# An mLSTM and stick-breaking trunk on eight cores: the sums of x, the first head's groups and the gate prologue rearranged, transposes planned with other due times

## The chip, the cores and the metric

The kernel runs on all 8 cores of one Trainium2 chip. Each core works on one of the 8 sequences of the batch and exchanges nothing with the others. The metric is the device time in microseconds (us) of the slowest core.

## The reference, cut to what matters

Two layers act on x of 2048 tokens by 2048 features per core.

Layer A (mLSTM, 8 heads): `u = x @ w_in` gives per head q and k (128 columns each), v (256), the output gate o and the SiLU gate z (256 each), and once for all heads 16 gate columns. q and k go through a causal convolution of width 4 and SiLU. The gate columns give a log input gate and a log forget gate per token and head; their running maxima and sums scale a chunkwise recurrence (here 16 chunks of 128 tokens per head) that mixes q, k and v. The result is normalised per head, multiplied by `sigmoid(o) * silu(z)`, projected by `w_out`, added to `alpha * x`, and layer-normalised.

Layer B (stick-breaking attention, 16 heads) projects queries, a SiLU gate and one shared set of keys and values, forms sigmoid scores with a running product along the keys, and ends with a projection, the residual and a layer norm.

## The kernel before, in words

**The planner.** The program is written as some 40 generators ("streams", all handed to `Sched.run`), each of which yields operations in its own order, with conditions between them. The planner keeps an estimated clock for each engine and for each tile (last written, last read) and emits, of all streams' next operations, the one whose estimated start is earliest; an operation marked `first=True` wins a tie. So the estimates don't move the hardware: they fix the order of the instructions in each engine's queue. The engines then run their queues in that order and wait by semaphores for true dependences. `slack` is added to the estimated end of whatever an operation waits for on another engine, so an operation with slack is put later in its queue. For DMAs (`KB.dma`) there is one estimated DMA clock `tdma`: each transfer, transposes too, starts after the one before it and takes `cost`; its destination counts as written, and its source as free, `lat` later. Transposes have `lat=LATE`, 14; all others 1.2.

**Queues.** Weights and x come by DMAs that GpSimd (POOL) issues, since they convert float32 to bfloat16. Transposes and stores are issued by SyncE (SP). Both queues are in order like any other.

**Layer A's beginning.** x arrives transposed in four blocks of 512 tokens, `XT[0..3]`. `plain` (matmul at L556) makes q, k and v of head 0 from it in the ordinary way: 4 x 64 matmuls of 512 columns into four PSUM banks, evicted by `pev` (L579). In between, `prologue` (L486) makes the gate columns of a block; after the fourth block it works out the gates for all heads: a chain that alternates between TensorE (L503, L507, L511, L513, L529) and VectorE (L505, L506, L509, L517, 32 dependent operations on one partition at L522 and L524, L526), with exponentials on ScalarE at L498, L500 and L535 to L538. Only after it (`st["pro"]`) may the recurrence of any head begin.

**Groups.** Every other projection of layer A is done by `grp` with 7 instead of 8 products (a Strassen form). A group is (head, pair pr of weight blocks, token half p): pr 0 is q and k, 1 is v, 2 and 3 are o and z. Weight pair `w = 4h + pr` sits in slot `w % 3` of `RW`; its loading starts once pair w-3 is done (`wd`). A group is 7 products of 8 matmuls (L608), 56 in all. Its operands are sums of weight quarters (`wsum`, L451: three on VectorE and two on POOL per pair) and sums of quarters of x (`xsum`, once per half p = 0, 1): three new tensors `FX` (L425, VectorE, 128x4096 bf16 each), two negations in place (L428, ScalarE) and two subtractions in place (L432, on POOL for p = 0, on VectorE for p = 1). `grp` waits until all seven of its half are in the queues (`at("xsum") >= p`), and `xsum` itself waits until all plain products and gates of the half are. The order is by the list `GL`: for head 0, whose q, k and v are already made, (o, p 0), (o, p 1), (z, p 0), (z, p 1). `gev` evicts a group (L626 to L683), with three subtractions or additions on VectorE.

**Beside the groups.** `conv` (L713 to L727) makes q and k of a head; `kn` transposes k, `vtr` transposes v by DMA; `knw` (L783), `recf` (L794), `recm` (L808 to L827) and `reco` (L840 to L853) do the recurrence chunk by chunk; `hbt` transposes its output by DMA into one of 12 tiles `HT`; `htg` (L869) multiplies by the gates that `gat` (L757 to L773) has made and stores to `mida`. The gates of head h+1 may overwrite those of head h only when the store of the same token block is issued. All DMAs have the line L162. After the last head the output projection of layer A starts (L941, tiles REGX and REGW), then layer B (L1104, L1185, L1212, L1238, L1270) and its output projection (L941 again, tiles REGH and REGX).

## Time and profile before

| what | us |
|---|---|
| three runs: median (lowest to highest) | 2592.64 (2577.12 to 2977.39) |
| profiled execution, device time | 2585.65 |
| its span, first to last instruction of the slowest core (core 3) | 2584.0 |
| spans of the eight cores | 2555.9 to 2584.0 |
| TensorE, VectorE, ScalarE, GpSimd busy in the span | 2439.5, 1729.4, 1031.0, 1262.1 |

The profiled execution's device time lies 1.65 us above its span. A window row of the profile gives, for one stretch of the span, the busy time and the number of records of each engine (PE is TensorE, DVE VectorE, ACT ScalarE), the granted TensorE clock as a share of full speed, the busy share of the DMA engines, and GB/s.

### The profile page before, as it was taken

To read this page: it belongs to the slowest core of one execution; us is meant where nothing else is said; L and a number is where in the kernel's file an instruction comes from. 1 tells how busy PE (TensorE), PEld (TensorE's weight loads), DVE (VectorE), ACT (ScalarE), POOL (GpSimd) and SP (SyncE) were. 2 spreads that over 40 slices of the span, in tenths; PEclk is the share of its full clock that TensorE was granted. 3 is DMA by queue.
4 is the path that set the end of the run, shared out by engine and by line. 5 is a ranking of instruction groups with operands and counts; after the bars stand their busy time and mean duration, and the time that the engine had idled before them with its cause. 6 is when DMAs were issued, how large, how long until landed. Compare 5 with 4: busy or idle time off the path is not lost.

```text
span 2584.0 us, 37351 instructions; the slowest of 8 cores (2555.9 to 2584.0 us)
## 1 busy us (share of the span) xinstructions
PE 2439.5 (94%) x11811; PEld 1127.4 (44%) x11811; DVE 1729.4 (67%) x2859; ACT 1031.0 (40%) x1877; POOL 1262.1 (49%) x1099
## 2 busy tenths in 40 slices
PE   7599899999999989999899999999999999998997
PEld 3244344444444444444344444444444444443443
DVE  2686687777778757664567766666666677565765
ACT  1455455555555532323334443433334444431111
POOL 2565465647557433433445544555444555442533
PEclk9799999999999989999899999999999999999998
DMA  9559766976567577973466576667767766686762
GB/s 155 81 80 89 107 101 108 111 122 111 96 113 113 93 255 231 252 216 80 111 114 134 105 131 113 124 118 122 123 114 109 115 109 102 133 195 175 252 202 82
DMA packets 518142, 342.35 MB, mean 132 GB/s; under 512 B 453184, under 2 KB 486080, under 8 KB 505536
## 3 DMA queue, kind: packets, MB, share of 16 engines
q1 hardware_dynamic: 492688, 214.06, 39.2%
q0 software_dynamic: 25264, 125.91, 27.7%
q8 instruction: 101, 1.65, 0.3%
q14 instruction: 89, 0.73, 0.1%
HBM read 272.82 MB, written 83.89 MB: 138 GB/s over the span
## 4 chain that ended last, share of the span: by engine, by line
PE 71%; DVE 11%; DMA 8%; POOL 4%; issue 4%; ACT 1%; SPq 1%; another core or an unknown queue 0%; DVEq 0%; POOLq 0%; ACTq 0%
PE PSA L1104 25%; PE PSA L608 19%; PE PSA L941 16%; PE PSA L1270 4%; DVE REGW L1212 4%; DMA REGX<-REGW 3%; PE PSA L1185 3%; DMA REGW<-a_wu 2%; PE PSA L556 2%; POOL REGW L1238 1%; DMA REGH<-REGX 1%; DVE REGW L451 1%; SPq L162 1%; DVE REGW L869 1%; DMA REGX<-x_t 1%
## 5 line engine op out<-in xcount | busy, mean ns | idle before, releaser
L1104 PE MATMUL PSA<-REGH,REGX 128*128 128x512 bf16 x4096 | 975.2, 380 | 5.9 <-DVE REGW L1111 5.9
L1212 DVE TENSOR_TENSOR_SCAN REGW<-PSA,REGW 128x512 f32<-128x512 f32 (+3 forms) x640 | 685.8, 1091 | 301.5 <-ACT PSA L1190 235.3
L1238 POOL TENSOR_TENSOR REGW<-REGW 128x1024 bf16<-128x1024 f32 (+7 forms) x384 | 526.9, 1389 | 354.0 <-DMA REGX<-REGW 185.0
L1104 PEld LDWEIGHTS PSA<-REGH,REGX 128*128 128x128 bf16 x4096 | 397.5, 98 | 461.6 <-issue 10.3
L1190 ACT ACTIVATE PSA<-PSA 128x512 f32<-128x512 f32 (+3 forms) x640 | 326.3, 519 | 304.0 <-PE PSA L1185 298.3
L608 PE MATMUL PSA<-REGX,REGW 128*128 128x512 bf16 x1680 | 405.8, 379 | 4.4 <-issue 3.6
L608 PE MATMUL PSA<-REGH,REGW 128*128 128x512 bf16 x1680 | 404.2, 382 | 0.0
L1116 ACT CAST REGW<-PSA 128x512 bf16<-128x512 f32 x192 | 112.7, 587 | 336.6 <-PE PSA L1104 334.9
L608 PEld LDWEIGHTS PSA<-REGH,REGW 128*128 128x128 bf16 x1680 | 163.8, 98 | 177.6 <-issue 4.7
L608 PEld LDWEIGHTS PSA<-REGX,REGW 128*128 128x128 bf16 x1680 | 160.9, 98 | 174.9 <-issue 5.9
L1185 PE MATMUL PSA<-REGW 128*128 128x512 bf16 (+3 forms) x640 | 220.1, 350 | 15.2 <-DVE REGW L1212 14.7
L941 PE MATMUL PSA<-REGH,REGX 128*128 128x512 bf16 x1024 | 223.8, 381 | 3.0 <-DVE REGW L944 2.0
L941 PE MATMUL PSA<-REGX,REGW 128*128 128x512 bf16 x1024 | 223.4, 382 | 0.0
L451 POOL TENSOR_TENSOR REGW<-REGW 128x1024 bf16<-128x1024 bf16 x60 | 132.4, 2212 | 58.2 <-DVE REGW L451 58.1
L848 POOL TENSOR_TENSOR REGW<-REGW,SM 128x1 f32<-128x1 f32 x128 | 76.9, 601 | 170.4 <-DVE REGW L846 153.4
L941 PEld LDWEIGHTS PSA<-REGH,REGX 128*128 128x128 bf16 x1024 | 100.5, 98 | 124.9 <-issue 5.9
L941 PEld LDWEIGHTS PSA<-REGX,REGW 128*128 128x128 bf16 x1024 | 100.7, 98 | 122.3 <-issue 2.7
L727 POOL TENSOR_TENSOR REGX<-REGW 128x512 bf16<-128x512 f32 x64 | 90.0, 1406 | 121.1 <-ACT REGW L725 82.0
L1270 PE MATMUL PSA<-REGX,REGW 128*128 128x512 bf16 (+3 forms) x640 | 130.6, 351 | 17.0 <-DMA REGX<-REGW 15.4
L964 ACT ACTIVATE REGW<-REGW,BMVB 128x2048 f32<-128x2048 f32 x26 | 54.3, 2093 | 229.4 <-DVE BMVB L958 229.4
L721 DVE SCALAR_TENSOR_TENSOR PSA<-REGW,PRT,PSA 128x512 f32<-128x512 f32 x128 | 96.1, 750 | 51.6 <-ACT PSA L715 49.7
L944 DVE SCALAR_TENSOR_TENSOR REGW<-REGW,PSA 128x512 f32<-128x512 f32 x108 | 73.9, 684 | 74.4 <-PE PSA L941 63.1
(144 smaller groups left out, 2440.5 us busy)
## 6 DMA issues: line engine op xcount, KB each, us to landing
REGW<-a_wu POOLq DMA_DIRECT2D x64, 512.0 KB, 8.1
y<-REGW SPq DMA_DIRECT2D x26, 1024.0 KB, 5.2
REGX<-wb POOLq DMA_DIRECT2D x32, 512.0 KB, 4.5
REGW<-y SPq DMA_DIRECT2D x14, 1024.0 KB, 7.6
REGW<-x SPq DMA_DIRECT2D x13, 1024.0 KB, 6.6
wao<-a_w_out POOLq DMA_DIRECT2D x32, 256.0 KB, 6.9
mida<-REGW SPq DMA_DIRECT2D x128, 64.0 KB, 2.8
wb<-kv_w POOLq DMA_DIRECT2D x32, 256.0 KB, 6.4
```

Of the source, the lines that this page charges most:

```text
L451: yield Op(e, lambda: E.tensor_tensor(out=out[0], in0=i0[0], in1=i1[0], op=op), R=i0[1] + i1[1], W=out[1], cost=x)
L608: yield Op("pe", lambda: P_.matmul(PS[bank], lhsT=wo[0][:, c, :], rhs=xo[0][:, c, :], start=(k == 0 and c == 0), stop=(c == 7), skip_group ...
L721: yield Op("dve", lambda: V.scalar_tensor_tensor(out=pc if k else acc, in0=U[u][:, k:k + 512], scalar=wk(k), in1=pc, op0=ALU.mult, op1=ALU ...
L727: yield Op("pool", lambda: G.tensor_tensor(out=dst[:, tb * 512:(tb + 1) * 512], in0=acc, in1=sig, op=ALU.mult), R=ak + gk, W=[dk[tb]], cos ...
L941: yield Op("pe", lambda: P_.matmul(PS[bank], lhsT=mg(c), rhs=wo[:, c, :], start=(c == 0), stop=(c == KC - 1)), R=mgk + wok, W=[("ps", bank ...
L1104: yield Op("pe", lambda c=c: P_.matmul(PS[bank], lhsT=WS[i % 4][:, c, :], rhs=X1[tb][:, c, :], start=(c == 0), stop=(c == KC - 1)), R=[f"W ...
L1116: yield Op("act", lambda: A_.copy(out=dstT[:, tsl], in_=PS[bank]), R=[("ps", bank)], W=[key], cost=0.6, first=True)
L1185: yield Op("pe", lambda: P_.matmul(PS[bank][:, 0:w], lhsT=QTs[par][:, (n - 1) * 128:n * 128], rhs=KTs[par][:, b0 * 128:b1 * 128], start=Tr ...
L1190: yield Op("act", lambda: A_.activation(out=PS[bank][:, 0:w], in_=PS[bank][:, 0:w], func=AF.Sigmoid, scale=-scale), R=[("ps", bank)], W=[( ...
L1212: yield Op("dve", lambda: V.tensor_tensor_scan(out=RR[slot][:, lo:hi][:, ::-1], data0=PS[bank][:, 0:w][:, ::-1], data1=mk[:, ::-1], initia ...
L1238: yield Op("pool", lambda: G.tensor_tensor(out=AA[:, (pos + b0) * 128:(pos + b1) * 128], in0=RR[slot][:, lo + 1:hi + 1], in1=RR[slot][:, l ...
L1270: yield Op("pe", lambda: P_.matmul(PS[bank][:, f0:512], lhsT=VVs[par][:, sb_, :], rhs=TT[:, gp + sb_, f0:512], start=(sb_ == 0), stop=(sb_ ...
```

## The change

It has eight parts.

1. `xsum`: the three new sums of a half are no longer held until all its plain products and gates are in the queues; each is held only until the first plain product of the last block that it reads is. The two subtractions of half 0 move from POOL to VectorE. None of the seven is `first` any more. Each enters a set `xs` by itself.
2. `grp`: a product waits for the one sum of x that it reads, `(p, k) in xs`, not for all seven.
3. `GL`: head 0's groups run (o, p 0), (z, p 0), (o, p 1), (z, p 1).
4. `wsum`: for weight pairs 2 and 3 all five sums are on VectorE.
5. `prologue`: five TensorE steps after the gates have slack 4.0 instead of 0.3.
6. `LATE` is 16 instead of 14.
7. `KB.dma`: transposes get an estimated clock of their own, `tsp`; they no longer delay, nor are delayed by, other transfers. A source counts as free `min(lat, 8)` after the transfer, the destination as written `lat` after it.
8. `hbt`: the output transposes have `lat` 32 for heads 0 to 6 and 12 for head 7.

```diff
-LATE = 14.0
+LATE = 16.0
+SLK = 4.0
...
-        self.tdma = max(self.tdma, start + 1.2) + cost
-        self._time(self.tdma + lat, R, W)
+        if lat > 1.2:
+            self.tsp = end = max(self.tsp, start + 1.2) + cost
+        else:
+            self.tdma = end = max(self.tdma, start + 1.2) + cost
+        self._time(end + min(lat, 8.0), R, ())
+        self._time(end + lat, (), W)
...
-            go = [(h, 2, 0), (h, 2, 1), (h, 3, 0), (h, 3, 1)] if h < NH_A - 1 else [(h, 2, 0), (h, 3, 0), (h, 2, 1), (h, 3, 1)]
+            go = [(h, 2, 0), (h, 2, 1), (h, 3, 0), (h, 3, 1)] if 0 < h < NH_A - 1 else \
+                [(h, 2, 0), (h, 3, 0), (h, 2, 1), (h, 3, 1)]
...
-                yield lambda: at("qkp") >= 4 * b + 3 and at("gates") >= b
...
-                for out, i0, i1, op in ((fx(0), b11, b22, ALU.add), (fx(2), b21, b11, ALU.subtract), (fx(1), b12, b22, ALU.subtract)):
+                for i, out, i0, i1, op, tb in ((1, fx(2), b21, b11, ALU.subtract, a), (0, fx(0), b11, b22, ALU.add, b),
+                                               (4, fx(1), b12, b22, ALU.subtract, b)):
+                    yield lambda: at("qkp") >= 4 * tb
...
-                             cost=2.3, first=True)
-                for x in (b22, b11):
...
+                             cost=2.3)
+                    xs.add((p, i))
+                yield lambda: at("qkp") >= 4 * b + 3 and at("gates") >= b
+                for i, x in ((2, b11), (3, b22)):
...
-                e, E, x = ("dve", V, 2.3) if p else ("pool", G, 7.5)
...
+                for i, out, i1 in ((5, b21, b22), (6, b12, b11)):
+                    yield Op("dve", lambda: V.tensor_tensor(out=out[0], in0=out[0], in1=i1[0], op=ALU.subtract), R=i1[1], W=out[1],
+                             cost=2.3)
+                    xs.add((p, i))
...
-                    e, E, x = ("pool", G, 2.2) if j > 2 else ("dve", V, 0.65)
+                    e, E, x = ("pool", G, 2.2) if j > 2 and w > 3 else ("dve", V, 0.65)
...
-                     R=["TRIU", "SPF"], W=[("ps", 6)], cost=0.25, slack=0.3)
+                     R=["TRIU", "SPF"], W=[("ps", 6)], cost=0.25, slack=SLK)
...
-                yield lambda: ((need is None and (3, pb) in evs or need in evd) and (w, sums) in ws and at("xsum") >= p)
+                yield lambda: ((need is None and (3, pb) in evs or need in evd) and (w, sums) in ws and (p, k) in xs)
...
-                         dma=dict(slot=f"ht{i % NHT}", out=HT[i % NHT], in_=HB[i % 4], transpose=True, lat=LATE))
+                         dma=dict(slot=f"ht{i % NHT}", out=HT[i % NHT], in_=HB[i % 4], transpose=True, lat=2 * LATE if i < 112 else LATE - 4))
```

## Rows read from the trace of the kernel before

**Rows 1.** The page, part 1 (TensorE's line), and spans of two cores
```profile
PE 2439.5 (94%) x11811; PEld 1127.4 (44%) x11811; DVE 1729.4 (67%) x2859; ACT 1031.0 (40%) x1877; POOL 1262.1 (49%) x1099
...
core 1: 2555.9 us, clock 0.983
...
core 3: 2584.0 us, clock 0.981
```

**Rows 2.** Line L941, layer A's output projection, core 1, then core 3
```profile
L941 PE MATMUL PSA<-REGX,REGW x1024: 379/379/631, 919.8 to 1142.9; 128*128 128x512 bf16 x171
...
L941 PE MATMUL PSA<-REGX,REGW x1024: 379/379/634, 944.7 to 1167.7; 128*128 128x512 bf16 x171
```

**Rows 3.** Windows of core 3, and last one of core 1
```profile
77.60:140.00 62.40, 31.88 (x131) 13.90 (x132) 51.22 (x97) 23.49 (x36) 26.80 (x17) 0.75 0.36 59
140.00:240.00 100.00, 98.45 (x489) 46.78 (x488) 75.81 (x196) 53.90 (x109) 57.45 (x64) 1.00 0.76 95
240.00:280.00 40.00, 27.73 (x121) 12.22 (x120) 17.74 (x48) 14.63 (x29) 18.92 (x18) 0.87 1.01 69
920.00:945.00 25.00, 16.55 (x81) 7.76 (x80) 15.08 (x53) 11.58 (x23) 9.80 (x12) 0.81 0.94 296
...
240.00:280.00 40.00, 40.00 (x202) 19.23 (x200) 31.93 (x83) 21.21 (x44) 29.77 (x30) 1.00 0.69 125
```

**Rows 4.** Timeline of TensorE: start, length, instructions [idle before, what ended it]
```profile
55.42 13.97 PE L556 MATMUL PSA<-REGH,REGW 128*128 128x512 bf16 x64
...
72.47 3.61 PE L556 MATMUL PSA<-REGH,REGW 128*128 128x512 bf16 x16
...
76.14 1.46 PE L556 MATMUL PSA<-REGH,REGW 128*128 128x512 bf16 x6
88.53 0.45 PE L507 MATMUL PSA<-ID,REGW 128*128 128x128 f32 x1 [10.94 <-DVE REGW L506]
...
101.44 1.19 PE L529 MATMUL PSA<-REGW,ONE 1*128 1x128 f32 x4 [8.05 <-DVE REGW L526]
...
111.71 0.59 PE L608 MATMUL PSA<-REGX,REGW 128*128 128x512 bf16 x2
...
120.20 0.27 PE L810 MATMUL PSA<-REGW 128*128 128x257 bf16 x1 [2.18 <-DVE REGW L797]
...
126.90 0.27 PE L794 MATMUL PSA<-REGX 128*128 128x128 bf16 x1 [6.08 <-ACT REGW L853]
```

**Rows 5.** Windows of L556 alone, then of L608 alone, TensorE and weight loads
```profile
77.60:140.00 62.40, 13.01 (x42) 4.58 (x42) 0.75 0.36 59
...
77.60:140.00 62.40, 15.57 (x61) 6.29 (x62) 0.75 0.36 59
```

**Rows 6.** Timeline of VectorE around the sums
```profile
56.64 6.69 DVE L425 TENSOR_TENSOR REGX<-REGX 128x4096 bf16<-128x4096 bf16 x3
...
72.65 0.62 DVE L495 TENSOR_TENSOR REGW<-PSA,REGW 128x128 f32<-128x128 f32 x2 [7.80 <-PE PSA L486]
...
77.93 8.01 DVE L451 TENSOR_TENSOR REGW<-REGW 128x1024 bf16<-128x1024 bf16 x3 [4.67 <-DMA REGW<-a_wu]
...
103.85 1.89 DVE L451 TENSOR_TENSOR REGW<-REGW 128x1024 bf16<-128x1024 bf16 x3
```

**Rows 7.** Line L451 on VectorE until 140 us: duration ns min/median/max, starts
```profile
L451 DVE TENSOR_TENSOR REGW<-REGW x7: 679/683/5739, 77.9 to 133.7; 128x1024 bf16<-128x1024 bf16 x7
```

**Rows 8.** Timeline of GpSimd
```profile
67.30 15.82 POOL L432 TENSOR_TENSOR REGX<-REGX 128x4096 bf16<-128x4096 bf16 x2 [10.78 <-ACT REGX L428]
...
90.38 0.59 POOL L162 DMA_DIRECT2D REGW<-a_wu  x1 [2.25 <-PE PSA L556]
```

**Rows 9.** Timelines of SyncE and ScalarE, then transposes of 200 to 300 us by median landing
```profile
237.46 9.93 SPq L162 DMA_TRANSPOSE REGH<-REGX  x1
...
269.64 0.40 ACT L783 ACTIVATE REGW<-REGH,REGW 128x128 bf16<-128x128 bf16 x1 [17.75 <-DMA REGH<-REGX]
...
REGW<-REGH SPq DMA_TRANSPOSE x8, 12.7
```

More of the change, by code:

```diff
@@ L507, in prologue @@
             yield Op("pe", lambda: P_.transpose(out=PS[7][:, 0:128], in_=AL, identity=ID32[:]), R=["AL", "ID32"],
-                     W=[("ps", 7)], cost=0.25, slack=0.3)
+                     W=[("ps", 7)], cost=0.25, slack=SLK)
             yield Op("dve", lambda: V.tensor_reduce(out=SM[:, 1:2], in_=PS[7][:, 0:128], axis=AX.X, op=ALU.max),
@@ L511, in prologue @@
             yield Op("pe", lambda: P_.matmul(PS[6][0:1, 0:128], lhsT=SM[:, 1:2], rhs=ID32[:], start=True, stop=True),
-                     R=["SM1", "ID32"], W=[("ps", 6)], cost=0.25, slack=0.3)
+                     R=["SM1", "ID32"], W=[("ps", 6)], cost=0.25, slack=SLK)
             yield Op("pe", lambda: P_.matmul(PS[6][0:1, 128:256], lhsT=ONE32[:, 0:1], rhs=SPF, start=True, stop=True),
@@ L529, in prologue @@
                 yield Op("pe", lambda: P_.matmul(PS[7][:, 128 * i:128 * i + 128], lhsT=ONE32[0:1, :], rhs=rw[:, 2 + i, :],
-                                                 start=True, stop=True), R=["ONE32", "ROW"], W=[("ps", 7)], cost=0.25, slack=0.3)
+                                                 start=True, stop=True), R=["ONE32", "ROW"], W=[("ps", 7)], cost=0.25, slack=SLK)
             yield Op("dve", lambda: V.tensor_tensor(out=TMP, in0=AL, in1=PS[7][:, 0:128], op=ALU.subtract),
```

11 lines of the change are left out of this document (4 added, 7 removed).

## The prediction, made before the changed kernel was run

> **What bounds the kernel now.** I read the busy shares first: TensorE is busy 94% of the span [rows 1], so the time is TensorE's work plus its holes. Next the spans of the cores: they do equal work, yet core 1 takes 2555.9 us and core 3, which sets the metric, 2584.0 [rows 1]. The first matmul of L941 ends layer A. On core 1 it starts at 919.8, on core 3 at 944.7 [rows 2]; from there to the end of the span it is 2555.9 - 919.8 = 1636 and 2584.0 - 944.7 = 1639 us. So all the spread arises in layer A, which is also all that the change touches, and the forecast can be made as: (start of L941 on the slowest core) + 1639 + 1.65 us around the span.
>
> Then windows of layer A [rows 3]. From 77.6 to 140 us TensorE is busy 31.88 of 62.40 us at a granted clock of 0.75. From 140 to 240 it is busy 98.45 of 100. From 240 to 280 core 3 loses 12.3 us, core 1 nothing. At the end, 920 to 945, 8.45 us are idle. So the beginning is the largest hole, and it is on every core.
>
> The timeline of TensorE names the waits of the beginning [rows 4]. By 77.6, 22 of the last block's 64 plain products are done (16 and 6). The 42 others are ready to run, but behind them in the queue's order come steps of the gate prologue: 10.94 us before L507, 8.05 before L529, both for VectorE. The first group's product starts at 111.71. Later 2.18 and 6.08 us (and 3.3 in two smaller ones) go to the recurrence, held while VectorE makes the sums of half 1. Why VectorE was late: its weight sums L451 take 8.01 us for three [rows 6]; their usual time is 0.683 us, but one took 5.739 [rows 7]. It began at 77.93 and ended near 83.7, just behind GpSimd's two subtractions, 67.30 to 83.12 [rows 8].
>
> **The change, part by part.**
>
> *Ceiling of the beginning.* Idle: 62.40 - 31.88 = 30.5 us [rows 3]. Slow clock: a plain product takes 13.97 / 64 = 0.218 us at full clock [rows 4]. The 42 plain ones took 13.01 instead of 9.2, the 61 of groups 15.57 instead of 13.3 [rows 5]: 6.1 us. Ceiling 36.6 us; no more can come from parts 1 to 5.
>
> *Sums of x (1, 2).* Each of the ten VectorE operations costs 6.69 / 3 = 2.23 us [rows 6]. For half 0 the three new sums used to run at 56.6 to 63.3 [rows 6] and can now go ahead of 56, where VectorE is mostly idle; its two subtractions, new on VectorE, cost 4.5 us and follow the negations, near 60 to 67. They lie beside plain products and cost nothing. For half 1, three new sums (6.7 us) can go at about 67 to 77, into the 7.80 and 4.67 us in which VectorE waited [rows 6]. If that cover is gone they fall on the prologue. Half 1's rest is 4.5 us behind its gates. Since a product waits only for its own sum, group 0 needs nothing of this that is late.
>
> *Weight sums (4).* Two pairs of two sums move to VectorE: 4 x 0.68 = 2.7 us. The 5.74 us operation goes back to 0.68 as the long subtractions leave GpSimd: -5.1 us. Pair 2 is complete at about 77.9 + 5 x 0.68 = 81.3. The Trainium skill (SBUF — State Buffer, "SBUF: two separate sides") says that VectorE and GpSimd take one pair of ports as an exclusive lock, the loser blocked for the whole instruction. The 5.74 us agree with that. By the same rule the sums moved to VectorE can block, or be blocked by, GpSimd's shorter multiplications; no term of my sum uses it.
>
> *Prologue slack (5).* A step is now put 4 us instead of 0.3 behind what it waits for, so plain products are issued ahead of it. VectorE can have its L506 result at about 81.3 + 1 = 82.3, against 76 + 5 = 81 by the planner's distance: a wait of about 1 us remains, between 0 and the 11 of before. The price is that the recurrence starts no earlier than now (L529 at 101) rather than earlier; while it is late, groups run.
>
> *Group order (3).* The 42 plain products from 77.6 end at 77.6 + 9.2 = 86.8, so group 0 can start near 87 instead of 111.7. A group is 56 x 0.218 = 12.2 us: group 1 at 99, group 2 at 111, group 4 at 136. Group 1 now needs pair 3. Its load waits for pair 0's last product; that was 90.38 [rows 8] and becomes about 80 to 81. Before, the pair's first sums ran at 103.85 [rows 6], 13.5 us behind the first load's issue; with that as an upper end and 3.4 for five sums it is ready by 98, 1 us ahead of need. If it came 5 us late, group 1 would lose 4; that is inside the range. Group 2 needs half 1's sums at 111, ready near 90. Pair 5's load starts after group 2 instead of group 1, 12 us later, and is needed 24 us after that: hidden.
>
> *Is VectorE able to follow?* This is what can eat the gain. Up to the work that is done by 240 us, VectorE is busy 51.22 + 75.81 = 127.0 us from 77.6 on [rows 3]. The change takes off 5.1 (block) and 6.7 (sums of half 1 made earlier), adds 2.7: 117.9 us. TensorE, given back its whole ceiling, would reach that work at 240 - 36.6 = 203.4, leaving VectorE 125.8 us: a busy share of 94%. In the crowded window before it had 51.22 / 62.40 = 82%. At 82% it would need 143.7 us, until 221.3, and the gain would be 18.7; at 94% all of 36.6. What VectorE does late is chiefly the recurrence, which may lag some chunks behind the groups without stopping TensorE, so I take a value nearer the ceiling: 30 us, bounds 18.7 and 36.6.
>
> *Due times in the steady part (6, 7, 8).* The trace shows no planned times, so these are bounds. In heads 1 to 7 TensorE has little left to give: 1.55 us in the 100 of the second window [rows 3]. Best: the hole of 240 to 280 goes too. It is 12.3 us idle and 27.73 x 0.13 = 3.6 of slow clock, 16 us. SyncE spent 9.93 us issuing one transpose at 237.46, and the k weighting on ScalarE waited 17.75 us for its landing [rows 9]. Worst: such a hole comes more often (rival 3). In a quiet queue a transpose is now due 2 us later than before; next to loads it is due earlier, as the planner no longer puts the loads' time in front of it. The rows show this collision of transposes and loads on core 3 only once, so I take 0, bounds -16 and +16. `lat` 32 for the output transposes puts L869 and the stores later in the queues; in tiles it has room (12 of them, against about 6.5 us per chunk), and nothing on TensorE waits for them until the end.
>
> *The tail (8).* Head 7's are due at 12 instead of 14, and no longer behind the three large loads of `w_out`. Between 0 and 8.45 us [rows 3] could go; the row shows work on the recurrence itself in that time, so 0.
>
> Sum: 2585.65 - 30 = 2555.65, say **2556 us**. The profiled execution lies 0.3% under the median shown, 2592.64, and between the other two runs' ends; I forecast against it.
>
> **The rivals.**
>
> 1. *VectorE takes TensorE's place at the beginning.* For it: 82% was the most it reached in 62 us, and every queue is in order. Against: its other 11.2 us there [rows 3] were mostly waits for TensorE's late steps, and those go. Time: 2585.65 - 18.7 = 2567.
> 2. *The hole at 240 us goes as well.* For it: core 1 has none in the same program, and the change shifts loads against transposes. Against: nothing in it thins the loads. Time: 2585.65 - 30 - 16 = 2540.
> 3. *Transposes planned too early next to loads: slower than before.* With a clock of their own, k and v transposes are planned as if no load ran. The rows show 12.7 us median landing for the v transposes of 200 to 300 us on core 3 and an issue of 9.93 [rows 9]. A TensorE step planned at such a due time stands in front of group products and stops them, 16 us each time. At one hole more per core, half of the 30 is gone; from two more on (-30 + 32) the kernel is slower. With three more in the seven heads: 2585.65 - 30 + 48 = 2604. Against: the due time was only roughly right before too, and one hole came of it. [...]
> 4. *The order doesn't change where it counts.* The planner may still estimate pair 2 or the gates so that the old order comes out. Against: slack and per-product conditions act on just the steps that waited. Time: 2586.
>
> **How the numbers follow.** Forecast 0.52, rival 1 0.20, rival 2 0.13, rival 3 0.08, rival 4 0.07. The forecast's own range is 2542 to 2570. Low end: 2585.65 - 36.6 - 16 - 8.45 = 2525 (say 2526); high end: rival 4 with some scatter of the runs, 2592, which leaves out rival 3. A measurement of this kernel can tell about 2% from no change, 2541 and 2644 here. Faster by over 2% are half of rival 2 and a tenth of the forecast: 0.11. Slower by over 2% is the far end of rival 3: 0.02. Within 2%: 0.87.
>
> **What would show it.** Right: TensorE's busy share from 77.6 to 140 above 0.9 at full granted clock; L608's first start near 87; waits before L507 and L529 under 2 us each; no VectorE L451 of 5 us; L432 four times on VectorE at 2.3 us; group products done by 140 near 210; L941 first starting near 915 on the slowest core and 890 on the best; 1639 us from there. Rival 1 would show as waits of TensorE for VectorE between 100 and 240, rival 3 as waits of ScalarE's L783 or TensorE for DMA in several heads. The forecast is wrong if L941 starts later than 935 on the slowest core, or if the part behind L941 changes.

## The result: slower, and where the profile shows it

Over 15 executions each, the kernel before had a median of 2572.76 us (2565.06 lowest) and the changed kernel 2622.51 us (2600.75 lowest). The ratio of the runs compared is **1.0166, 95% interval 1.0142 to 1.0190**. The forecast was 2556 us, in a range of 2526 to 2592; the result lies outside it, on the other side of the kernel before. Runs that were disturbed on a whole die are left out of all ratios here.

The profiled execution of the changed kernel took 2600.75 us. It was the fastest of its 15, while the profiled one of before (2585.65) lay above its median. So the two traces differ by only 15 us where the ratio says some 40; the traces tell where time goes, the ratios how much, and what the changed kernel loses in its slower executions no trace here shows. The page and the spans of the two cores of [rows 1]:

```profile
PE 2444.6 (94%) x11811; PEld 1127.0 (43%) x11811; DVE 1736.0 (67%) x2865; ACT 1033.4 (40%) x1879; POOL 1232.0 (47%) x1093
...
core 1: 2587.9 us, clock 0.985
...
core 3: 2599.1 us, clock 0.982
```

Most lines of the kernel moved down by 9: L608 is now L617 (groups), L556 L565, L503 L512, L507 L516, L529 L538, L451 L460, L853 L862, L869 L878, L941 L950. L162 and L432 are L167 and L440. In the experiments without part 7 they lie 1 to 4 lines higher. Layer A's output projection on core 3, against 944.7 in [rows 2]:

```profile
L950 PE MATMUL PSA<-REGX,REGW x1024: 379/379/634, 955.5 to 1184.1; 128*128 128x512 bf16 x171
```

For every core I split the span at three events: the first group product, the last one, and the first output-projection product. Medians over the eight cores, us:

| kernel | first group | groups' stretch | tail | behind it | span |
|---|---|---|---|---|---|
| before | 111.3 | 810.8 | 11.7 | 1638.3 | 2571.1 |
| changed | 91.8 | 841.9 | 7.9 | 1641.2 | 2582.2 |

The columns are, in order: start of the first group product, from it to the last one, from there to the first product of the output projection, from there to the end, and the whole.

**The beginning did gain; the groups lost more than that.** They start 19.5 us sooner and then take 31.1 us longer. Both halves show in the windows of core 3, the first three of which answer to [rows 3]; the last row of the fence behind it is the kernel before over the long steady stretch:

```profile
77.60:140.00 62.40, 53.91 (x243) 24.06 (x242) 47.68 (x111) 35.62 (x55) 22.73 (x22) 0.92 0.41 66
140.00:240.00 100.00, 85.71 (x421) 40.36 (x418) 67.77 (x183) 47.43 (x99) 50.99 (x58) 0.96 0.85 99
240.00:280.00 40.00, 33.19 (x161) 15.53 (x162) 34.13 (x91) 20.36 (x41) 23.66 (x26) 0.90 0.58 88
...
280.00:880.00 600.00, 565.48 (x2763) 265.72 (x2762) 465.39 (x1121) 305.30 (x618) 336.78 (x365) 0.99 0.69 105
```

```profile
280.00:880.00 600.00, 585.42 (x2897) 277.39 (x2895) 475.10 (x1178) 320.57 (x650) 358.42 (x385) 1.00 0.69 110
```

TensorE is busy 22.0 us more up to 140 us, 12.7 less in the next hundred, and 19.9 less from 280 to 880. No single wait of the steady stretch is large; that is why it must be read by windows and groups of waits.

**Beginning, core 3.** L565 alone, then L617 alone, from 77.6 to 140 us, against [rows 5]; then TensorE, VectorE and ScalarE in the timelines, against [rows 4, 6]:

```profile
77.60:140.00 62.40, 11.31 (x44) 4.41 (x42) 0.92 0.41 66
...
77.60:140.00 62.40, 40.86 (x171) 16.78 (x172) 0.92 0.41 66
```
```profile
83.01 0.46 PE L512 MATMUL PSA<-REGW 128*128 128x128 f32 x2 [2.75 <-ACT REGW L509]
...
91.79 1.89 PE L617 MATMUL PSA<-REGX,REGW 128*128 128x512 bf16 x8
99.42 2.29 PE L617 MATMUL PSA<-REGX,REGW 128*128 128x512 bf16 x5 [5.74 <-ACT PSA L635]
```
```profile
80.57 4.28 DVE L460 TENSOR_TENSOR REGW<-REGW 128x1024 bf16<-128x1024 bf16 x5
```
```profile
92.17 1.28 ACT L734 ACT_TABLE_LOAD   x1 [7.50 <-DVE REGW L730]
...
95.18 3.61 ACT L437 ACTIVATE REGH<-REGH 128x4096 bf16<-128x4096 bf16 x1
98.69 0.58 ACT L635 COPY PSA<-PSA 128x512 f32<-128x512 f32 x1
```

The waits of 10.94 and 8.05 us before L507 and L529 (L516, L538) are gone, and so is the 5.74 us weight sum; 2.75 us are left before L512. By 140 us 171 group products have run where there had been 61: 110 x 0.218 = 24 us of lead. A new wait of 5.74 us stands in the first group. Its eviction L635 sits in ScalarE's queue behind a table load and the 3.61 us negation L437 of half 1's sums. VectorE has a part in it: ScalarE had stood 7.50 us for VectorE's L730, which came behind five weight sums (4.28 us from 80.57) and these two sums of half 1:

```profile
84.77 4.49 DVE L432 TENSOR_TENSOR REGH<-REGH 128x4096 bf16<-128x4096 bf16 x2
```

**Head 1, core 3.** Part of the chain of waits, then lines of VectorE's, TensorE's and SyncE's timelines:

```profile
215.88 26.53 DMA REGW<-a_wu
```
```profile
242.43 0.69 DVE L460 TENSOR_TENSOR REGW<-REGW 128x1024 bf16<-128x1024 bf16 x1 [15.38 <-DMA REGW<-a_wu]
```
```profile
244.51 0.27 PE L803 MATMUL PSA<-REGX 128*128 128x128 bf16 x1 [15.19 <-ACT REGW L862]
```
```profile
216.60 12.53 SPq L167 DMA_TRANSPOSE REGW<-REGH  x1
...
234.39 11.24 SPq L167 DMA_TRANSPOSE REGW<-REGH  x1
```

A weight load issued at 215.88 took 26.5 us to land, beside transposes whose issue alone took 12.5 and 11.2 us. VectorE had the pair's first sum next in its queue and stood for 15.4 us; the recurrence's steps behind it, and so TensorE, stood too. It is the hole of [rows 3] with another victim: there a transpose was late for ScalarE, here a load for VectorE. From 200 to 280 us TensorE is idle 12.4 us in the mean over the cores, where it was 7.0 before.

**Heads 2 to 7, core 0.** TensorE's recurrence lines between 280 and 880 us, first before, then changed. The last part is idle time ahead of them and what ended it (the same lines, 9 apart):

```profile
L808 PE MATMUL PSA<-REGW 128*128 128x257 bf16 x92 | 25.1, 273 | 3.2 <-DVE REGW L822 2.2 <-ACT REGW L783 0.7
L810 PE MATMUL PSA<-REGW 128*128 128x257 bf16 x92 | 25.1, 273 | 6.6 <-DVE REGW L797 4.8 <-DVE REGW L841 1.6
...
L794 PE MATMUL PSA<-REGX 128*128 128x128 bf16 x91 | 19.9, 219 | 0.6 <-ACT REGW L853 0.3
```
```profile
L819 PE MATMUL PSA<-REGW 128*128 128x257 bf16 x87 | 23.8, 274 | 8.4 <-DVE REGW L806 7.1 <-DVE REGW L854 0.8 <-DVE REGW L859 0.3
L817 PE MATMUL PSA<-REGW 128*128 128x257 bf16 x86 | 23.5, 273 | 8.8 <-DVE REGW L831 8.1 <-ACT REGW L792 0.8
...
L803 PE MATMUL PSA<-REGX 128*128 128x128 bf16 x86 | 18.8, 219 | 5.5 <-ACT REGW L862 5.3
```

10.4 us became 22.7: 3.2 + 6.6 + 0.6 against 8.4 + 8.8 + 5.5. Most of it is for VectorE, and the 5.3 for ScalarE's L862 too come from its waiting for VectorE's L859 (46.7 us in all there). Two pictures from head 4 of that core show why VectorE is late. The first is a load that VectorE waits for; the second, operations of two engines that hold each other up:

```profile
585.37 0.69 DVE L460 TENSOR_TENSOR REGW<-REGW 128x1024 bf16<-128x1024 bf16 x1 [3.03 <-DMA REGW<-a_wu]
...
586.60 0.27 PE L817 MATMUL PSA<-REGW 128*128 128x257 bf16 x1 [1.78 <-DVE REGW L831]
```
```profile
596.62 3.18 DVE L878 TENSOR_TENSOR REGW<-REGW 128x256 bf16<-128x256 bf16 x2
...
597.48 2.17 POOL L460 TENSOR_TENSOR REGW<-REGW 128x1024 bf16<-128x1024 bf16 x1
...
601.58 0.27 PE L819 MATMUL PSA<-REGW 128*128 128x257 bf16 x1 [1.69 <-DVE REGW L806]
```

Two small multiplications that otherwise take 0.48 us took 3.18, beside the end of a GpSimd multiplication (L773, until 597.51) and GpSimd's sum. From these rows I formed the theory for the experiments: *with the new due times the order of the queues is wrong by some microseconds in every head; VectorE's next instruction waits for a load, or meets a long GpSimd operation, and the recurrence stands behind it.* The idle time in heads 2 to 6 supports it: most of it lies at the same four chunks. At chunk 15 it is 1.2 to 1.7 us in every head and on every core; at chunks 6, 8 and 12 the mean over the cores is 0.1 to 2.4 us by head, with none on some cores. A fixed order gives such a pattern; chance alone would not.

### The profile page after: what moved, and what is told of

The parts are those of the page before. It is cut to its first block, busy times and chain, and to the rows that moved or that the text cites. A ratio compares the mean times of both kernels' runs of the same rounds, so it can differ in the third digit from the quotient of the medians.

```text
span 2599.1 us, 37395 instructions; the slowest of 8 cores (2566.7 to 2599.1 us)
## 1 busy us (share of the span) xinstructions
PE 2444.6 (94%) x11811; PEld 1127.0 (43%) x11811; DVE 1736.0 (67%) x2865; ACT 1033.4 (40%) x1879; POOL 1232.0 (47%) x1093
## 4 chain that ended last, share of the span: by engine, by line
PE 71%; DVE 12%; DMA 8%; issue 4%; POOL 3%; ACT 2%; SPq 1%; DVEq 0%; POOLq 0%; ACTq 0%
PE PSA L1113 26%; PE PSA L617 18%; PE PSA L950 16%; DVE REGW L1221 5%; PE PSA L1279 4%; PE PSA L1194 3%; DMA REGW<-REGW 3%; DMA REGW<-a_wu 2%; DMA REGX<-REGW 2%; PE PSA L565 1%; DMA REGX<-x_t 1%; DVE REGW L878 1%; POOL REGW L1247 1%; SPq L167 1%; DVE REGW L460 1%
## 5 line engine op out<-in xcount | busy, mean ns | idle before, releaser
L617 PE MATMUL PSA<-REGX,REGW 128*128 128x512 bf16 x1680 | 406.5, 382 | 6.0 <-ACT PSA L635 5.7
L617 PE MATMUL PSA<-REGH,REGW 128*128 128x512 bf16 x1680 | 407.7, 382 | 2.8 <-DVE REGW L859 2.8
L617 PEld LDWEIGHTS PSA<-REGX,REGW 128*128 128x128 bf16 x1680 | 162.9, 98 | 178.9 <-issue 12.7
L617 PEld LDWEIGHTS PSA<-REGH,REGW 128*128 128x128 bf16 x1680 | 162.8, 98 | 177.4 <-issue 6.1
L950 PE MATMUL PSA<-REGX,REGW 128*128 128x512 bf16 x1024 | 223.9, 382 | 5.1 <-DVE REGW L953 5.1
L950 PE MATMUL PSA<-REGH,REGX 128*128 128x512 bf16 x1024 | 223.8, 381 | 2.4 <-DVE REGW L953 1.5
L736 POOL TENSOR_TENSOR REGX<-REGW 128x512 bf16<-128x512 f32 x64 | 84.4, 1319 | 165.7 <-ACT REGW L734 111.6
L950 PEld LDWEIGHTS PSA<-REGX,REGW 128*128 128x128 bf16 x1024 | 100.8, 99 | 128.0 <-issue 8.9
L950 PEld LDWEIGHTS PSA<-REGH,REGX 128*128 128x128 bf16 x1024 | 100.4, 98 | 124.4 <-issue 5.5
L1279 PE MATMUL PSA<-REGX,REGW 128*128 128x512 bf16 (+3 forms) x640 | 130.6, 351 | 15.5 <-DMA REGX<-REGW 13.8
L460 POOL TENSOR_TENSOR REGW<-REGW 128x1024 bf16<-128x1024 bf16 x56 | 123.5, 2205 | 29.0 <-DVE REGW L460 28.8
L862 ACT ACTIVATE REGW<-PSA,REGW 128x256 bf16<-128x256 f32 x128 | 71.6, 559 | 118.7 <-DVE REGW L859 102.7
```

Of the source, the lines that this page charges most:

```text
L460: yield Op(e, lambda: E.tensor_tensor(out=out[0], in0=i0[0], in1=i1[0], op=op), R=i0[1] + i1[1], W=out[1], cost=x)
L617: yield Op("pe", lambda: P_.matmul(PS[bank], lhsT=wo[0][:, c, :], rhs=xo[0][:, c, :], start=(k == 0 and c == 0), stop=(c == 7), skip_group ...
L736: yield Op("pool", lambda: G.tensor_tensor(out=dst[:, tb * 512:(tb + 1) * 512], in0=acc, in1=sig, op=ALU.mult), R=ak + gk, W=[dk[tb]], cos ...
L950: yield Op("pe", lambda: P_.matmul(PS[bank], lhsT=mg(c), rhs=wo[:, c, :], start=(c == 0), stop=(c == KC - 1)), R=mgk + wok, W=[("ps", bank ...
L1279: yield Op("pe", lambda: P_.matmul(PS[bank][:, f0:512], lhsT=VVs[par][:, sb_, :], rhs=TT[:, gp + sb_, f0:512], start=(sb_ == 0), stop=(sb_ ...
```

## The experiments

Ratios are to the kernel before, with their 95% intervals. "Parts 1 to 5 alone" (e1) is the base of most.

### Halves of the change

e1 is the changed kernel without parts 6, 7, 8:

```diff
-LATE = 16.0
+LATE = 14.0
...
-        if lat > 1.2:
-            self.tsp = end = max(self.tsp, start + 1.2) + cost
-        else:
-            self.tdma = end = max(self.tdma, start + 1.2) + cost
-        self._time(end + min(lat, 8.0), R, ())
-        self._time(end + lat, (), W)
+        self.tdma = max(self.tdma, start + 1.2) + cost
+        self._time(self.tdma + lat, R, W)
...
-                         dma=dict(slot=f"ht{i % NHT}", out=HT[i % NHT], in_=HB[i % 4], transpose=True, lat=2 * LATE if i < 112 else LATE - 4))
+                         dma=dict(slot=f"ht{i % NHT}", out=HT[i % NHT], in_=HB[i % 4], transpose=True, lat=LATE))
```


> Parts 1 to 5 alone: the due times of transposes (LATE 14, one DMA clock, output transposes like all) are those of before. Theory 1 (the new due times cost time in heads 1 to 7, the new beginning gains its share): first group product near 92 us as in the changed kernel, waits of TensorE for the recurrence from 280 us on as short as before (about 10 us instead of 25), time 0.99 to 0.995 of before. Theory 2 (the lead won at the beginning is itself what disturbs the later heads, through VectorE or through the order of the queues): first group product near 92, but the later heads as slow as in the changed kernel, time 1.01 to 1.02 of before.

e2 is the kernel before with exactly these lines changed the other way (parts 6, 7, 8 alone).

> Parts 6 to 8 alone on the kernel before. Theory 1: the beginning as before (first group product near 111 us), longer waits of TensorE in heads 1 to 7, time 1.02 to 1.03 of before, slower than the changed kernel. Theory 2: the time of before within 0.5%.

e1: **0.9923** [0.9878, 0.9967]; e2: **1.0081** [1.0058, 1.0103]. The beginning's parts make the kernel faster, the due times make it slower, and that settles where the sign comes from. The stage table: e1 97.5 / 793.8 / 11.7 / 1638.3, e2 101.9 / 824.8 / 7.5 / 1649.1. e1's groups take 17 us less than before, e2's 14 us more. The split is not clean: the due times alone (e2) also start the groups 9.4 us sooner, and behind the groups e2 loses 10.8 us. The product of the two ratios is 1.000, the whole is 1.0166; 1.6% are an interaction.

### One part of the due times taken away from the changed kernel

e3 takes the last edit of e1's diff alone (part 8 undone), e4 the middle one alone (part 7 undone).

> The changed kernel without part 8: the output transposes are due LATE (16) after their transfer for all heads, not 32 and 12. If part 8 is what costs (products and stores L878 put late in VectorE's queue, gates held up behind them): the time falls to 0.99 to 1.00 of before. If part 7 or the beginning costs: it stays within 0.5% of the changed kernel, 1.012 to 1.02.

> The changed kernel without part 7: one estimated DMA clock for transposes and loads, sources free as late as destinations are written; LATE 16 and the 32 and 12 of part 8 stay. If transposes planned too early beside loads are what costs (rival 3 of the prediction): the time falls to 0.99 to 1.00 of before. If not: it stays at 1.012 to 1.02, or rises a little, since output tiles count as busy for 32 us more.

e3: 1.0049 [1.0010, 1.0089]; e4: **1.0468** [1.0418, 1.0518]. So part 8 costs, and removing part 7 alone is far worse than keeping it. In e4 the output transposes have `lat` 32 and their source tile `HB`, of which there are four, counts as taken for 32 us. The planner then spaces the recurrence by it. Core 0 of e4, TensorE from 280 to 880 us:

```profile
L815 PE MATMUL PSA<-REGW 128*128 128x257 bf16 x76 | 22.8, 300 | 44.5 <-DVE REGW L802 43.4 <-DVE REGW L846 0.5 <-DVE REGW L855 0.4
...
L799 PE MATMUL PSA<-REGX 128*128 128x128 bf16 x75 | 17.4, 232 | 15.2 <-ACT REGW L858 15.2
```

Part 8 can stand only where a source is freed apart from the landing, as part 7 does (8 us) and as e10 below does (14 us); the three parts can't be judged one at a time.

### One part of the due times added to parts 1 to 5

e5 and e11 change `LATE` alone, to 16.0 (part 6) and 15.0. e6 adds the whole of part 7. e7 adds only its early release of the source, e8 only the clock of its own, e10 part 8 with the sources free after 14 as in e1:

```diff
 e7
+        self.tdma = end = max(self.tdma, start + 1.2) + cost
+        self._time(end + min(lat, 8.0), R, ())
+        self._time(end + lat, (), W)
 e8
+        if lat > 1.2:
+            self.tsp = end = max(self.tsp, start + 1.2) + cost
+        else:
+            self.tdma = end = max(self.tdma, start + 1.2) + cost
+        self._time(end + lat, R, W)
 e10
+        self._time(self.tdma + min(lat, 14.0), R, ())
+        self._time(self.tdma + lat, (), W)
...
+                         dma=dict(slot=f"ht{i % NHT}", out=HT[i % NHT], in_=HB[i % 4], transpose=True, lat=32.0 if i < 112 else 12.0))
```


> The new beginning with the due times of before, but LATE 16 (part 6 alone of the three). If 2 us more on every transpose cost nothing, the time is that of the beginning alone, 0.985 to 0.997 of before, the groups' stretch about 794 us (median over cores, first to last group product). If a due time that is later costs much by itself (LATE is part of what made the groups' stretch 842 in the changed kernel), the stretch is over 810 and the time above 1.0.

> The new beginning with LATE 14 and part 7 whole: a DMA clock of its own for transposes, and sources free 8 us after the transfer. If part 7 is what made the groups' stretch long (rival 3 of the prediction, in this or that form), it is 820 to 840 and the time about 1.0 to 1.01 of before; if LATE 16 was, it is about 794 and the time 0.99.

> The new beginning with LATE 14, one DMA clock as before, but sources counted as free min(lat, 8) after the transfer instead of lat (half of part 7). If the early release is what costs (the output chunks HB are written, and with them the recurrence steps of TensorE are placed, as if the transposes had read their sources 6 us sooner), the groups' stretch is over 815. If the separate clock costs, it stays near 794.

> The new beginning with LATE 14, sources free as late as before, but a DMA clock of its own for transposes (the other half of part 7). If transposes planned as if no load ran are what costs, the groups' stretch is over 815 and there are more waits for transposes to land; if the early release costs, it stays near 794.

> The new beginning with the due times of before, and part 8 alone: output transposes due 32 (head 7: 12) after their transfer instead of 14, their sources still free after 14. Part 8 was seen to cost about 8 us of the groups' stretch on top of parts 6 and 7. If that is additive: groups' stretch about 802 us, time 0.995 to 1.0 of before. If each part costs its whole alone, as parts 6 and 7 did (any departure from the old order costs): stretch 815 or more, time 1.0 or more.

> The new beginning with LATE 15, half way to part 6. If the time follows the due time smoothly: between 0.992 and 1.001 of before. If what decides is the chance of how the planner's order falls (VectorE's operations against GpSimd's that block them), it can lie outside, 1.005 or 0.987 as well.

| run | ratio | interval | groups' stretch |
|---|---|---|---|
| e1 base | 0.9923 | 0.9878 to 0.9967 | 793.8 |
| e11, LATE 15 | 0.9922 | 0.9895 to 0.9950 | 790.8 |
| e5, LATE 16 | 1.0014 | 0.9973 to 1.0055 | 814.7 |
| e6, all of part 7 | 1.0031 | 1.0002 to 1.0060 | 827.4 |
| e7, early release | 1.0060 | 1.0024 to 1.0095 | 838.8 |
| e8, own clock | 1.0055 | 1.0020 to 1.0090 | 827.7 |
| e10, part 8 | 0.9980 | 0.9952 to 1.0009 | 808.2 |

Parts 6 and 7, and either half of part 7, take the whole gain back, each on its own. For part 8 the intervals of e10 and e1 overlap; its groups' stretch is 14 us longer. The waits for DMAs from 280 to 880 us on core 0 show how; columns are the total, how often, the longest. First e7, then e8, then the changed kernel without part 8 (e3):

```profile
DVE REGW L457 <- DMA REGW<-a_wu: 25.2, 9, 8.0
ACT REGW L859 <- DMA REGW<-REGW: 12.1, 4, 3.9
```
```profile
ACT REGW L791 <- DMA REGH<-REGX: 18.3, 3, 8.1
DVE REGW L459 <- DMA REGW<-a_wu: 17.5, 8, 3.9
```
```profile
ACT REGW L862 <- DMA REGW<-REGW: 32.5, 6, 15.5
```

Before and in e1 there is one such row, weight loads:

```profile
DVE REGW L451 <- DMA REGW<-a_wu: 8.0, 8, 1.8
```
```profile
DVE REGW L456 <- DMA REGW<-a_wu: 3.0, 4, 1.2
```

With early release (e7, e3) ScalarE is told to write `HB` (L859, L862) while the transpose still reads it. With an own clock (e8) the k weighting (L791) stands before its transpose has landed. In both, the loads' sums stand too early on VectorE: 25 and 17.5 us against 3.0. The k weighting's wait is not found in the changed kernel: there L792 waits for no transpose between 280 and 900 us, on any core.

### The loads, and both due times moved back

Both start from the changed kernel. e9 has the first edit (the planned length of a weight load), e13 both:

```diff
-                yield Op("pool", None, W=rwk[s][2 * u:2 * u + 2], cost=3.0,
+                yield Op("pool", None, W=rwk[s][2 * u:2 * u + 2], cost=4.5,
...
-        self._time(end + min(lat, 8.0), R, ())
+        self._time(end + min(lat, 14.0), R, ())
```

> The changed kernel, with a weight load planned at a cost of 4.5 instead of 3.0 us, so that the weight sums (VectorE, in order) are put later. Theory: part 7 took the transposes out of the loads' estimated clock, weight sums are now put in VectorE's queue before their weights have landed, and what is behind them (the recurrence, then TensorE) waits. Then VectorE's waits for a_wu in heads 2 to 7 fall from 15 us to about 7 (kernel before: 6), the idle time of TensorE there from 31 to about 23, the time to 1.005 to 1.01 of before. Rival, that the transposes' own due times or GpSimd's blocking of VectorE are the cause: the waits for a_wu fall, but the idle time and the time stay (1.012 or more).

> The changed kernel with weight loads planned at 4.5 us as before this, and with the sources of transposes counted as free 14 us after the transfer instead of 8. Theory: two kinds of waits on DMAs made the later heads long, VectorE's weight sums for a_wu, and ScalarE's output chunk (L862) for the transpose that still reads its tile. Both should now be near 0 and TensorE's idle time in heads 2 to 7 fall from 31 us (25 without the first) to 10 to 15, the time to 0.995 of before. If it stays at 24, DMA waits are not the second half, and GpSimd's blocking of VectorE or the order itself is.

e9: 1.0062 [1.0034, 1.0090]; e13: 1.0090 [1.0060, 1.0119]. e9's edit did what it should: the waits for `a_wu` between 280 and 900 us are gone (16.8 us on core 0 before the edit), and a percent comes back. e13's second edit did not: ScalarE's L862 still waits 5.6 us for transposes in the mean over the cores (6.2 in the changed kernel), though the blocked sums shrink. Means over the cores (us), the first three from the first group product of head 2 to the last of head 7: TensorE idle, VectorE waiting for `a_wu`, what VectorE's weight sums take above 0.683 us each; then TensorE waiting in layer A's output projection for `mida`, which it reads back:

| kernel | idle | waits for a_wu | sums' excess | wait for mida | ratio |
|---|---|---|---|---|---|
| before | 10.9 | 6.4 | 9.1 | 0 | 1 |
| changed | 31.7 | 14.9 | 16.5 | 0 | 1.0166 |
| e1 | 11.7 | 7.1 | 8.9 | 0 | 0.9923 |
| e2 | 34.1 | 19.8 | 14.6 | 0 | 1.0081 |
| e10 | 20.8 | 6.5 | 12.5 | 0 | 0.9980 |
| e11 | 7.7 | 5.1 | 18.2 | 0 | 0.9922 |
| e9 | 25.0 | 0.0 | 12.7 | 18.7 | 1.0062 |
| e13 | 17.1 | 0.5 | 3.5 | 17.0 | 1.0090 |
| e12 (below) | 8.3 | 4.3 | 2.1 | 0 | 0.9882 |

Neither cause alone sets the idle time: e9 has no wait for a load left and 25.0 us idle, and e11 has the largest excess of the table and the least idle time. That the two together make up the holes is therefore argued from the rows above, not shown.

e13 cures some two thirds of what the steady part had lost, yet its ratio is no better than e9's. One reason stands in the last stage. Both kernels reach the output projection early and then stand in it, on every core by 14.8 to 21.6 us. TensorE and SyncE of core 0 in e9:

```profile
920.59 3.61 PE L950 MATMUL PSA<-REGX,REGW 128*128 128x512 bf16 x16 [1.42 <-DMA REGW<-mida]
943.94 4.42 PE L950 MATMUL PSA<-REGX,REGW 128*128 128x512 bf16 x10 [19.73 <-DMA REGW<-mida]
...
935.91 2.49 SPq L167 DMA_DIRECT2D REGW<-mida  x3
```

Three of its reads of `mida` are issued at 935.91 only, behind transposes and stores in SyncE's queue, when the projection has already begun. In the kernel before, core 0, they were issued by 927.2 and the projection began at 935.6. So what the edits win in the heads is partly paid again here; the planned length of a load moves this order too. e8 has 7.8 us of the same wait. The other reason is a lower clock, see e17 below.

### The slack, the order of groups, the engines of the sums

e12 and e18 are e1 without the added slack (parts 1 to 4 alone), e14 is e12 with `LATE` 15.0, e16 is e12 without part 3, e17 is the changed kernel without the added slack. e15 is the kernel before with only the two engine choices of parts 1 and 4:

```diff
-SLK = 4.0
+SLK = 0.3
...
-            go = [(h, 2, 0), (h, 2, 1), (h, 3, 0), (h, 3, 1)] if 0 < h < NH_A - 1 else \
+            go = [(h, 2, 0), (h, 2, 1), (h, 3, 0), (h, 3, 1)] if h < NH_A - 1 else \
...
-                e, E, x = ("dve", V, 2.3) if p else ("pool", G, 7.5)
+                e, E, x = ("dve", V, 2.3)
...
-                    e, E, x = ("pool", G, 2.2) if j > 2 else ("dve", V, 0.65)
+                    e, E, x = ("pool", G, 2.2) if j > 2 and w > 3 else ("dve", V, 0.65)
```


> The new beginning with the due times of before, without part 5: the prologue's TensorE steps have slack 0.3 again. By the prediction part 5 frees the plain products: without it two waits come back, before the second and the last prologue step, smaller than 10.9 and 8.1 us since VectorE's weight sum is no longer blocked; about 10 us together, first group product at about 105 instead of 98, time about 0.4% above the new beginning alone, 0.996 of before. If the freeing of VectorE did it all, the time is unchanged, 0.992.

> The fastest kernel so far (the new beginning without part 5, due times of before) with LATE 15. A candidate for the best, and a second sight of how smooth LATE is: if 1 us of due time does nothing, 0.988 as without it; if the planner's order falls by chance, anything from 0.98 to 1.0.

> The kernel before with one thing changed: half 0's two subtractions and the weight sums of pairs 2 and 3 on VectorE (no early sums, no conditions per product, old group order). By the prediction's reading, VectorE's weight sum was late by 5.1 us through GpSimd's 15.8 us subtractions: the first 10.94 us wait of TensorE shrinks to about 5, the 8.05 one stays or moves; time 0.995 to 0.998 of before. If it makes most of the beginning's gain by itself: 0.99.

> The new beginning without part 5, due times of before, and without part 3: head 0's groups in the old order, half 1 second. By the prediction part 3 gives half 1's sums 12 us more: without it group 1 comes at about 112 us, its sums are ready at about 90 if VectorE follows, so nothing is lost: 0.988. If VectorE is behind there, TensorE waits again some 5 to 8 us for half 1's sums between 105 and 130 us: 0.991.

> The changed kernel with SLK 0.3, parts 6 to 8 kept. The two halves of the change measured alone multiply to 0.992 x 1.008 = 1.000, the whole is 1.0166; 1.6% are an interaction. Theory (the slack is what interacts: it puts the recurrence of head 0 later, and the loads and the early transposes of head 1 then meet in the hole of 200 to 280 us): ratio to before 1.000 or less (0.9882 x 1.008 = 0.996), head 1's idle time of 12.5 us on the median core falls under 5, the stretch of the groups from 841.9 to 822 or less. Rival (the interaction lies in heads 2 to 7, between transposes' due times and whatever order layer A is in): the slack is worth only the 0.4% that it is worth without parts 6 to 8, ratio 1.012, head 1 stays above 9 us.

> The kernel of e12 once more (parts 1 to 5, slack 0.3, the old due times), in more rounds, as it is the fastest so far. If its gain is real: ratio 0.988 again, between 0.985 and 0.991. If e12 had a lucky draw: 0.992 as in e1.

e12: **0.9882** [0.9858, 0.9906]; e18, the same kernel in more rounds: **0.9909** [0.9871, 0.9946]. e14: 0.9959 [0.9919, 0.9999]; e15: 0.9955 [0.9909, 1.0000]; e16: 1.0006 [0.9945, 1.0066]; e17: **1.0016** [0.9981, 1.0050].

The kernel with parts 1 to 4 and no added slack beats both kernels. Core 3 of e12, windows and TensorE's timeline:

```profile
77.60:140.00 62.40, 53.56 (x259) 25.57 (x260) 53.58 (x144) 36.86 (x67) 22.56 (x25) 0.95 0.49 75
...
240.00:280.00 40.00, 38.64 (x198) 18.62 (x196) 31.45 (x90) 21.69 (x44) 32.09 (x32) 1.00 0.57 101
280.00:880.00 600.00, 593.98 (x2941) 281.89 (x2940) 470.62 (x1195) 327.81 (x665) 355.63 (x381) 1.00 0.64 110
```
```profile
81.26 0.30 PE L512 MATMUL PSA<-ID,REGW 128*128 128x128 f32 x1 [0.85 <-DVE REGW L511]
...
92.57 1.19 PE L534 MATMUL PSA<-REGW,ONE 1*128 1x128 f32 x4 [5.94 <-DVE REGW L531]
```

Without the slack TensorE stands 5.9 us for the 32 dependent operations, and the first group starts at 100.2 (median over the cores), 2.7 us later than in e1, which has the slack, and 8.4 later than in the changed kernel. But the step that had waited 10.94 us as L507 [rows 4], here L512, waits 0.85: the longest wait was cured by parts 1 and 4, not by the slack. e15, which has only the two engine choices of parts 1 and 4, shows the same without any reordering: L507 waits 0.92 us there, L529 6.12, and the ratio is 0.9955. The groups of e12 take 791.5 us instead of 841.9, but nearly all of that is the due times: e1 has 793.8.

**The slack is what interacts.** e17 keeps parts 6 to 8 and drops only the slack: 1.0166 becomes 1.0016. TensorE's idle time from 200 to 280 us, where head 1's hole is, falls from 12.4 to 1.1 us in the mean over the cores, while in heads 2 to 7 it stays (31.7 and 35.8). The theory had asked for a ratio of 1.000 or less, head 1 under 5 us and a stretch of 822 or less; the first is met within the interval, the second clearly, the third not (829.8). The rival had head 1 staying above 9, and is out. The hole is 11 us of the 1.5%, which is 39 us; where the rest went was not found, as the changed kernel's trace is of its fastest execution. So the hole of head 1 belongs to the slack together with the due times, the small holes of heads 2 to 7 to the due times alone.

**A lower clock on a pair of cores.** e17's profile also explains much of e16 and part of e13. In its profiled execution six cores have the same course from 100 to 240 us and cores 2 and 3 another. Windows of core 0, then of core 2:

```profile
75.00:85.00 10.00, 2.02 (x6) 0.98 (x6) 6.91 (x11) 4.41 (x8) 2.65 (x2) 0.71 0.46 89
...
100.00:240.00 140.00, 137.36 (x686) 65.52 (x685) 117.06 (x290) 83.76 (x165) 79.12 (x86) 1.00 0.63 97
```
```profile
75.00:85.00 10.00, 1.32 (x6) 0.78 (x5) 6.16 (x9) 4.41 (x8) 2.65 (x2) 0.75 0.55 95
...
100.00:240.00 140.00, 138.83 (x566) 61.70 (x577) 96.79 (x240) 69.71 (x136) 61.93 (x70) 0.81 0.58 87
```

Core 2 is busier and does 566 matmuls where core 0 does 686: the granted clock is 0.81, between the full level and the half one. On both cores TensorE had been nearly idle from 75 to 85 us and had begun again at the low clock. The stretch at 0.81 begins near 95 us and ends near 250; it costs (1 - 0.81) x 155 = 29 us. Other profiled executions show it too: e16 on cores 2 and 3, e18 on 4 and 5, e13 on 2 to 5; the others none. It takes two neighbouring cores each time (e13: two such pairs), and not the same ones in each execution of a kernel. Where a run has such a pair (both mean clocks 0.006 or more under the kernel's median), its slowest core is later:

| kernel | slowest span without such a pair (runs) | with one (runs) |
|---|---|---|
| e12 | 2555 (4) | none |
| e18 | 2548 (2) | 2570 (4) |
| e16 | 2556 (2) | 2586 (5) |
| e14 | 2566 (3) | 2575 (3) |
| changed | 2612 (8) | 2619 (3) |
| e17 | 2590 (6) | 2613 (1) |
| before, run beside e9 to e12 | 2584 (14) | none |
| before, run beside e13 to e16 | 2572 (8) | 2589 (6) |
| before, run beside e17 and e18 | 2580 (14) | 2595 (7) |

The groups of runs were made on different chips, so spans compare only within a group. e16 without the pair has 2556 against 2572 for the kernel before, 0.994; e12 has 2555 against 2584, 0.989. So e16's 1.0006 is mostly the pair and says little against the old group order; two runs are too few to price part 3. By the same reckoning e15 comes to 0.998, and e18 to 0.987. e13's cores without it span 2553 to 2564 in its profile, against 2567 to 2599 in the changed kernel. The kernel is not what decides it: the kernel before has 13 low pairs of 140 beside e13 to e18, and none of 216 beside e1 to e12. In the same late groups e16 has 5 of 28, e15 1 of 32, and all five compared runs of e13 have low cores, so the kernel may have a part in it as well; that is not shown.

## Why the prediction was wrong, by its own steps

**The step that failed is "due times in the steady part: I take 0".** Parts 6 to 8 cost 0.8% on the kernel before (e2) and 2.4% on top of parts 1 to 5 (1.0166 / 0.9923), some 20 to 60 us where I allowed ±16. I reasoned that heads 1 to 7 had little left to give and looked for large holes like the one at 240 us. The loss came in small waits, chiefly at four chunks of a head: 20.8 us more idle time of TensorE in heads 2 to 7 (31.7 against 10.9), and 5.4 more from 200 to 280 us. Rival 3 had the right sign and a chance of 0.08. The loss that it priced, 2604 against 2585.65 or 18 us, was under half of the 43 that the ratio shows. Its mechanism shows in e8, where L791 waits 18.3 us for transposes on core 0; the sign that I named for it, such waits in several heads, is absent from the changed kernel behind 280 us. There the weight loads' sums stood too early, and the early release of sources, which I had not priced at all, let ScalarE come to write tiles that transposes still read. The hole at 240 us, which I expected either to stay or to go, grew on the changed kernel (15.2 us of wait) and became smaller in e12: from 200 to 280 us, 3.1 us idle in the mean over the cores against 7.0 before.

The sum also started from the profiled execution of before, 2585.65, where the median of before is 2572.76; that put the forecast in us 13 too high, which hid part of the miss.

**The step "prologue slack, part 5" failed in sign.** I credited the slack with freeing the plain products. e12 shows that VectorE, once relieved, is in time by itself (0.85 us). The wait before L529 did cost as I said, 5.9 us without slack; but taking the slack away, for which I had named only the price that "the recurrence starts no earlier", gains 1.5% in e17 against the changed kernel. In e12 against e1 it is only 0.4%, inside the intervals.

**The size of the beginning was near, in part by luck.** Of 30 us, 24 are there at 140 us and 19.5 in the start of the groups; but I had credited parts 1 to 5 with it, and alone (e1) they start the groups only 13.8 us sooner. The due times, which I had put at nothing there, brought the other 5.7. Group 0 started at 91.8 and not near 87; L516 and L538 had no wait in the timeline, as asked (under 2 us). What is missing from 30 at 140 us is one wait of 5.74 us that I had not listed, before the first group's eviction: ScalarE's negation, itself late by a wait for VectorE. TensorE's share in the window was 0.86 at clock 0.92, where I had asked for 0.9 at full clock; 171 group products, where I had said near 210. L432 (L440) ran four times on VectorE at 2.28 us each, and no weight sum took 5 us there. Parts 1 to 5 as a whole gave 0.8%, 20 us of the 30, by the interval 8 to 31.

**Right:** L941 as the point from which the rest is constant in the changed kernel (1641 against 1638 us; 1643.6 on core 3; not so in e9 and e13), the 5.74 us operation as a block by GpSimd, and VectorE as able to follow on the whole (rival 1: its 76% share at the beginning was below the 82% of before), save for the 7.50 us that ScalarE stood for it. **The tail** gave 3.8 us, where I took 0 of 8.45. One of the signs of failure that the prediction named came true: L950 first starts at 955.5 on the slowest core, past the 935 named.

**VectorE beside GpSimd.** Two L878 took 3.18 us beside GpSimd's L773 and L460, against 0.48 alone; and the weight sums' excess falls from 16.5 to 3.5 us between the changed kernel and e13, where only the order changed. The Trainium skill (SBUF — State Buffer, "SBUF: two separate sides") says that VectorE and GpSimd take one pair of ports as an exclusive lock, the loser blocked for the whole instruction. These rows agree, also where I had used the rule for no term. What the excess is worth in time is another matter: e11 has 18.2 us of it at 0.9922.

**Open.** Why the release of sources and the own clock do no more harm together (e6, 1.0031) than either alone (1.0060, 1.0055), and why part 8 costs little on e1 (0.6%, intervals overlap) and 1.2% on the whole. What brings the 0.81 clock. The stretch behind L941 varies between 1637 and 1661 us among kernels whose code there is the same: in e9, e13 and e8 the waits for `mida` (18.7, 17.0 and 7.8 us) account for most of it; why it is 1651 in e11 and 1649 in e2, which have no such wait, is open.

## What to carry to other kernels

In a list-scheduled kernel an estimated due time is a tuned constant, not a model of the transfer. Making it more plausible in one place (a clock of its own, a source freed sooner) shifts every queue by microseconds, in every head, and in these runs the fixed order turned that into small waits that no single row shows; try such edits one at a time, against windows of the steady stretch, and look at the next stage too: e9 and e13 lost behind the groups what they had won in them. Remove the cause of a wait first (here the VectorE work ahead of it), and only then see whether reordering around it still pays. And when a variant comes out slower by about one percent, compare the cores' granted clocks before blaming the edit.

## What the runs showed of the hardware that I had not expected

- A granted clock of 0.81 for about 155 us on two neighbouring cores, in some executions of a program and not in others, with the six other cores at 0.98 to 1.00 from 100 to 240 us (e16, e17, e18); the slowest span is 22 to 30 us longer with it in e18 and e16, 15 to 17 in the kernel before, 7 in the changed one.
- A weight load took 26.5 us to land, and one transpose's issue held SyncE for 12.5 us, when both met in head 1.
- A pair of 128x256 multiplications on VectorE took 3.18 us beside a 1.09 us GpSimd multiplication and a 2.17 us GpSimd sum, against 0.48 alone.
